# Mixture-of-experts in 64-row blocks, two side by side on the halves of TensorE's columns, the second block's weights copied to a fixed place by VectorE

## Chip, cores and metric

One core of one Trainium2 chip. The metric is the device time in microseconds of one execution; the median of three runs stands for a kernel. All data are fp32.

## What is computed

Two layers of a hybrid backbone over 512 latent and 256 context tokens of width 1024. Each layer has a token mixer (windowed attention, gated DeltaNet, latent attention) and then a mixture of experts. Layer 0 sends all 768 tokens through the experts, layer 1 only the 512 latent ones. The change lies in the experts:

```
swiglu(t, wg, wu, wd) = (silu(t @ wg) * (t @ wu)) @ wd      # 1024 -> 256 -> 1024
top_idx, top_w = route(h)          # 8 of 64 experts per token
for each expert: y = swiglu(rows that chose it); routed[token] += weight * y
out = swiglu(h, shared weights) + routed
```

The given inputs fix the routing. Of layer 0's 6144 rows, 12 experts get at most 64, 40 get 65 to 128, and 12 get 129 to 192. Of layer 1's 4096 rows the same three classes hold 41, 17 and 5 experts, and one expert has 219. In blocks of 128 rows of one expert that is 76 and 70 blocks; in blocks of 64 it is 128 and 94.

## The kernel before

Rows are sorted by expert into blocks of 128 rows (`phase_tail` computes, on the chip, a table `plan` with the expert of every block and the index list `idx`). `phase_experts` then runs a loop on each engine over pairs of blocks, `r = 0, 1`. A block goes through these steps:

- POOL gathers 128 rows of 1024 from DRAM (`gather`, L2214), two blocks ahead; TensorE turns them (`turn`, 8 transposes, L2227), ScalarE copies them to `xT` (L2282).
- `gate_up(r)` (L2233): 8 matmuls, 128 rows x 512 columns of gate and up weights, which TensorE takes as 16 passes. ScalarE applies silu, VectorE multiplies by the up half into `hid` (L2327, L2331), `turn_hidden` (L2239) turns it, VectorE copies it to `hT` (L2329, L2333).
- `down(r, n)` (L2244): 4 matmuls, 8 passes. ScalarE copies the left half of the result, VectorE the right half (L2338), ScalarE's queue stores 512 KB to `y_slots`.

TensorE's order in a pair is: gate_up(0), turn(0), gate_up(1), turn_hidden(0), turn(1), turn_hidden(1), down(0), down(1).

The weights of expert `e` (2 MB gate and up, 1 MB down) lie in slot `e % 4` of a ring `W` of `WRING = 4` slots. SP loads them in order of the experts; three are loaded before the loop. A slot is free when the last block of expert `e - 4` has ended: SP waits for `blocks_done`, which the last matmul of `down(r, 1)` raises, against the table `T_FREE`. One expert has at least one block, so a pair of blocks touches at most two experts, and the other two slots can be filled ahead.

The modulation product (L241) already uses groups of TensorE's columns: 8 matmuls with 2 stationary columns each, on column groups starting at 0, 32, 64 and 96 in turn, all with 128 rows and 512 moving columns of their own.

Of the kernel before, what the change touches and what calls it, by code (L numbers as in the profile page):

```python
# [50 lines left out]
BIG = 1e30  # L51

# [4 lines left out]


# [127 lines left out]
ARENA_WORDS = 53200  # L186
# [4 lines left out]
def plan_at(nq):  # L191

    n = nq * TOPK + NE + 2
    return n, 2 * n, 2 * n + NE + 1


def build(nc, A, out):
# [8 lines left out]
    NBMAX = NT + NT * TOPK + NE  # L206
# [3 lines left out]
    with outer:  # L210
# [48 lines left out]
        FIXED = max(b for a, b in arena.used)  # L259
        ROOMS = (NT * GCH + 6 * NTOK, (4 + 2 * MH) * NTOK + NT * MH * HD)  # L260
# [140 lines left out]
        def front_rows(featroom):  # L401

            first = carve(featroom)
            return first(NT, D), first(D), first(2, D)


        class Next:
# [3 lines left out]
            def __init__(self, stack):  # L411
                nq = NLT
                sizes = [nq * TOPK, nq * TOPK, nq * TOPK + NE + 2, plan_at(nq)[2], NT * 12, ROOMS[0], NT * W_VB, ROOMS[1]]
                self.at = max(b for a, b in arena.used if b <= FIXED) + sum(n + n % 2 for n in sizes)
                self.hT = sbuf(stack, "hT", [P, DK, NTOK], place=self.at)
                self.wt = arena.tensor[0:P, self.at + DK * NTOK:self.at + DK * NTOK + DK * 384]
                self.sems = Sems(nc, "next")
                self.x_out, self.w_in = self.sems("x_out"), self.sems("w_in")


        def phase_front(l, nq, vb, featroom, lateroom, X, x_in, nxt):
# [4 lines left out]
            xt, sq, hh = front_rows(featroom)  # L426
# [15 lines left out]
            with st:  # L442
# [43 lines left out]
                with nc.Block() as block:  # L486
# [306 lines left out]
                    def _(pe):  # L793
                        def item(it):
# [4 lines left out]
                            if kind == "chan":  # L799
                                c, jj = a // 3, a % 3  # L800
                                pe.wait_ge(w_in[c], 16)
                                w = wt[:, WOFF[c]:WOFF[c] + DK * 384].rearrange("p (k n) -> p k n", n=384)
# [793 lines left out]
        def phase_tail(l, nq, ob, W, dest, wk, idx, plan, route_keep, xg, gathered, xT, xT_ready, sz, w_in, c_in, T):  # L1596
# [6 lines left out]
            NB = nq * TOPK + NE  # L1603
            NBC = NB + 2
            T_SLOT, T_FREE, T_END = plan_at(nq)
# [5 lines left out]
            with st:  # L1611
# [32 lines left out]
                cmpb = sbuf(st, "cmpb", [NE, P])  # L1644
# [5 lines left out]
                bo = [ap[:, 0:TOPK * NB].rearrange("p (k n) -> p k n", n=NB) for ap in (xt[2], tt)]  # L1650
# [21 lines left out]
                with nc.Block() as block:  # L1672
# [168 lines left out]
                    def _(pe):  # L1841
# [94 lines left out]
                        def block_experts():  # L1936
                            pe.wait_ge(cmp_ready, 1)
                            nc.tensor.matmul(psum[0:1, 1, 0:P], cst("ones")[0:NE, 0:1], cmpb[:, :], start=True, stop=True).then_inc(be_done, 1)

                        def slot_tokens(i):  # L1940
# [3 lines left out]
                            for k in range(TOPK):  # L1944
                                n = i * TOPK + k
                                last = nc.tensor.matmul(psum[:, 0, 0:NB], po[:, i % 2, k], bo[i % 2][:, k], start=(n == 0), stop=(n == nq * TOPK - 1))
# [53 lines left out]
                    def _(dve):  # L2000
# [102 lines left out]
                        for j in range(1, nq):  # L2103
                            ch(V.scalar_tensor_tensor(out=nblk[:, :], in0=cnt, scalar=j * P + 0.5, in1=nblk[:, :], op0=ALU.is_gt, op1=ALU.add))
# [4 lines left out]
                        ch(V.tensor_scalar(tmpe[:, :], tmpe[:, :], float(P), nq * P + 1.0, ALU.mult, ALU.add))  # L2109
# [17 lines left out]
                        V.tensor_scalar(cmpb[:, :], cst("iota")[0:NE], ecol[:, 0:1], None, ALU.is_ge).then_inc(cmp_ready, 1)  # L2127
# [3 lines left out]
                        for i in range(nq):  # L2131
                            if i >= 2:
                                dve.wait_ge(hot_used, i - 1)
                            V.tensor_tensor(po[:, i % 2], cst("iota").unsqueeze(1).to_broadcast([P, TOPK, P]),
                                            p8[:, i].unsqueeze(2).to_broadcast([P, TOPK, P]), ALU.is_equal)
                            V.tensor_tensor(bo[i % 2], cst("iota")[:, 0:NB].unsqueeze(1).to_broadcast([P, TOPK, NB]),
                                            b8[:, i].unsqueeze(2).to_broadcast([P, TOPK, NB]), ALU.is_equal).then_inc(same_ready, 1)
                        ch(V.memset(idx[:, NB:NBC], 0))
# [3 lines left out]
                        V.tensor_copy(idx[:, 0:NB], psum[:, 0, 0:NB]).then_inc(idx_done, 1)  # L2142

                        ch(V.memset(bf[:, NB:NBC], float(NE)))
                        ch(V.tensor_scalar(bf[:, T_SLOT:T_SLOT + NBC], bf[:, 0:NBC], -1.0, None, ALU.add))
                        ch(V.tensor_copy(qi[:, :], bf[:, T_SLOT:T_SLOT + NBC]))
                        ch(V.tensor_scalar(qi[:, :], qi[:, :], WRING - 1, None, ALU.bitwise_and))
                        ch(V.tensor_copy(bf[:, T_SLOT:T_SLOT + NBC], qi[:, :]))
                        ch(V.tensor_scalar(bf[:, T_SLOT:T_SLOT + NBC], bf[:, T_SLOT:T_SLOT + NBC], float(WSLOT), None, ALU.mult))
# [3 lines left out]
                        ch(V.tensor_scalar(plan[:, T_END - 1:T_END], plan[:, T_END - 1:T_END], 1, None, ALU.logical_shift_right))  # L2153
# [6 lines left out]
        def phase_experts(l, nq, W, idx, plan, xs, ys, wk, route_keep, xg, gathered, xT, xT_ready):  # L2160
            NB = nq * TOPK + NE
            T_SLOT, T_FREE, T_END = plan_at(nq)
            st, S = ExitStack(), Sems(nc, f"ex{l}")
            with st:
                sg = sbuf(st, "sg", [P, 2, DE])
                hid = sbuf(st, "hid", [P, 2, DE])
                hT = sbuf(st, "hTe", [P, 2, DE])
                yb = sbuf(st, "yb", [P, 2, D])
                w_in = [S(f"w_in{r}") for r in range(WRING)]
                y_out = [S("y_out0"), S("y_out1")]  # L2170
                step = S("step")
                w_ready, blocks_done = S("w_ready"), S("blocks_done")
# [3 lines left out]
                rows_in = S("rows_in")  # L2176
                LEFT, RIGHT = (5, 7), (6, 5)

                def used_pairs(eng):

                    return eng.value_load(plan[0:1, T_END - 1:T_END], min_val=0, max_val=NB // 2)

                with nc.Block() as block:
                    @block.sync
                    def _(sp):
                        sp.sem_inc(w_ready, 3)
                        for e in range(3, NE):
                            r = e % WRING
                            if e >= WRING:
                                free = sp.value_load(plan[0:1, T_FREE + e - WRING:T_FREE + e - WRING + 1], min_val=1, max_val=NB + 1)  # L2190
                                sp.wait_ge(blocks_done, free)
                            sp.dma_start(W[:, r * WSLOT:r * WSLOT + DK * 2 * DE],
                                         A["w_gu"][l * (NE + 1) + 1 + e].rearrange("p k n -> p (k n)")).then_inc(w_in[r], 16)
                            sp.dma_start(W[:, r * WSLOT + DK * 2 * DE:(r + 1) * WSLOT],
                                         A["w_dn"][l * (NE + 1) + 1 + e].rearrange("p k n -> p (k n)")).then_inc(w_in[r], 16)
                            if e > 3:
                                before = e - 1
                                sp.wait_ge(w_in[before % WRING], 32 * (before // WRING + (before % WRING == 3)))
                                sp.sem_inc(w_ready, 1)
                        sp.wait_ge(w_in[(NE - 1) % WRING], 32 * (NE // WRING))  # L2200
                        sp.sem_inc(w_ready, 1)
                        sp.dma_start(xs[:, :, :], xres[0:nq * P, :].rearrange("(i p) d -> p i d", p=P)).then_inc(rows_in, 16)
                        sp.dma_start(ys[:, :, :], y_dram[0:nq * P, :].rearrange("(i p) d -> p i d", p=P)).then_inc(rows_in, 16)
# [4 lines left out]
                    def _(pool):  # L2208
# [9 lines left out]
                        for j in range(NB // 2):  # L2218
# [5 lines left out]
                    def _(pe):  # L2224
# [5 lines left out]

                        def gate_up(r, slot):
# [456 lines left out]
```

## Time and profile before

| | |
|---|---|
| median of 3 runs | 3626.09 us (3623.57 to 3629.45) |
| profiled execution, span | 3630.5 us |
| TensorE busy | 3384.4 us, 93% of the span |
| weight loads of TensorE | 1937.8 us, 53% |
| VectorE, ScalarE busy | 1088.2 us, 891.0 us |
| mean granted clock of TensorE | 0.964 of 2.4 GHz |
| HBM | 776.58 MB moved, mean 214 GB/s |

The span runs from the first to the last instruction of one profiled execution. No device time is shown apart from the span for that execution; its span is 4.4 us (0.12%) above the median of the runs. The expert loops take 981 to 1873 us (layer 0) and 2743 to about 3570 us (layer 1) of it.

### The profile page before, as it was taken

To read this page: it belongs to the slowest core of one execution; us is meant where nothing else is said; L and a number is where in the kernel's file an instruction comes from. 1 tells how busy PE (TensorE), PEld (TensorE's weight loads), DVE (VectorE), ACT (ScalarE), POOL (GpSimd) and SP (SyncE) were. 2 spreads that over 40 slices of the span, in tenths; PEclk is the share of its full clock that TensorE was granted. 3 is DMA by queue.
4 is the path that set the end of the run, shared out by engine and by line. 5 is a ranking of instruction groups with operands and counts; after the bars stand their busy time and mean duration, and the time that the engine had idled before them with its cause. 6 is when DMAs were issued, how large, how long until landed. Compare 5 with 4: busy or idle time off the path is not lost. (4 is left out here: it accounts for less than half of the span.)

```text
span 3630.5 us, 59980 instructions
## 1 busy us (share of the span) xinstructions
PE 3384.4 (93%) x22912; PEld 1937.8 (53%) x22913; DVE 1088.2 (30%) x2570; ACT 891.0 (25%) x1790; POOL 513.5 (14%) x568
## 2 busy tenths in 40 slices
PE   7998979989899999999987998899898999999996
PEld 4545659845444444444433555679544444444442
DVE  3424534445311111111125435434442111111114
ACT  2323432222211111111124224422221111111112
POOL 0100024220100000000024010052311000000003
PEclk8998989999999999999999999999899999999998
DMA  9603310123288886978867103200335999999965
GB/s 381 266 9 121 136 49 4 62 108 155 106 318 327 325 351 226 363 294 328 330 264 254 64 9 130 71 3 4 144 151 199 366 365 366 362 363 362 356 242 220
DMA packets 147619, 776.58 MB, mean 214 GB/s; under 512 B 25952, under 2 KB 43872, under 8 KB 110688
## 3 DMA queue, kind: packets, MB, share of 16 engines
q1 hardware_dynamic: 88960, 560.92, 39.7%
q0 software_dynamic: 33120, 120.60, 9.5%
q10 hardware_dynamic: 25344, 92.29, 6.2%
q8 instruction: 143, 2.34, 0.3%
q14 instruction: 52, 0.43, 0.0%
HBM read 637.44 MB, written 136.31 MB: 213 GB/s over the span
## 5 line engine op out<-in xcount | busy, mean ns | idle before, releaser
L2233 PE MATMUL psum<-arena 128*128 x2336 | 1037.5, 597 | 15.7 <-issue 15.7
L2233 PEld LDWEIGHTS psum<-arena 128*128 128x128 f32 x2336 | 433.8, 191 | 555.7 <-issue 555.7
L2244 PE MATMUL psum<-arena 128*128 x1168 | 515.3, 594 | 0.0
L810 PE MATMUL psum<-arena 128*128 128x480 f32 (+3 forms) x1088 | 401.5, 525 | 13.2 <-PEq L152 5.2
L2214 POOL DMA_INDIRECT arena<-h,arena x146 | 137.6, 943 | 1527.8 <-PE psum L2227 1503.7
L2244 PEld LDWEIGHTS psum<-arena 128*128 128x128 f32 x1168 | 215.9, 190 | 244.5 <-issue 244.4
L2294 ACT ACTIVATE arena<-psum 128x256 f32<-128x256 f32 x146 | 56.2, 385 | 1032.3 <-PE psum L2233 1032.3
L810 PEld LDWEIGHTS psum<-arena 128*128 128x128 f32 x1088 | 206.7, 193 | 186.8 <-issue 175.4
L2338 DVE COPY arena<-psum 128x512 f32<-128x512 f32 x146 | 101.0, 692 | 422.0 <-PE psum L2244 422.0
L2329 DVE COPY arena<-psum 128x256 f32<-128x256 f32 x73 | 31.0, 425 | 519.9 <-PE psum L2239 519.9
L2327 DVE TENSOR_TENSOR arena<-arena,psum 128x256 f32<-128x256 f32 x73 | 30.7, 421 | 488.0 <-ACT arena L2294 488.0
L2282 ACT COPY arena<-psum 128x1024 f32<-128x1024 f32 x146 | 147.9, 1013 | 87.2 <-PE psum L2227 87.2
L2301 ACT COPY arena<-psum 128x512 f32<-128x512 f32 x146 | 85.7, 587 | 291.2 <-PE psum L2244 291.2
L2227 PEld LDWEIGHTS psum<-arena 128*128 128x128 f32 x1168 | 134.4, 141 | 38.5 <-issue 38.5
L2227 PE MATMUL psum<-arena 128*128 128x128 f32 x1168 | 151.4, 273 | 0.0
L1864 PE MATMUL psum<-arena 128*128 128x512 f32 x320 | 143.1, 606 | 0.0
L996 PE MATMUL psum<-arena 128*128 128x64 f32 x896 | 120.1, 279 | 20.7 <-ACT arena L1108 20.2
L996 PEld LDWEIGHTS psum<-arena 128*128 128x128 f32 x896 | 109.5, 192 | 55.5 <-ACT arena L1108 40.0
L1432 DVE TENSOR_TENSOR arena<-psum,arena 128x384 f32<-128x384 f32 x120 | 66.9, 558 | 151.1 <-PE psum L1330 139.7
L2490 PE MATMUL psum<-arena 128*128 128x512 f32 x160 | 89.1, 658 | 22.4 <-DMA arena<-y_slots,arena 17.6
L2407 POOL DMA_INDIRECT arena<-y_slots,arena x80 | 88.2, 1103 | 107.1 <-POOLq L152 81.4
L1864 PEld LDWEIGHTS psum<-arena 128*128 128x128 f32 x320 | 61.6, 195 | 75.2 <-issue 75.2
(350 smaller groups left out, 3812.5 us busy)
## 6 DMA issues: line engine op xcount, KB each, us to landing
arena<-in_w_gu SPq DMA_DIRECT2D x130, 2048.0 KB
arena<-in_w_dn SPq DMA_DIRECT2D x130, 1024.0 KB
y_slots<-arena ACTq DMA_DIRECT2D x156, 512.0 KB
arena<-in_ada SPq DMA_DIRECT2D x24, 2048.0 KB
y_slots<-arena SPq DMA_DIRECT2D x8, 4096.0 KB
arena<-in_w_gdn SPq DMA_DIRECT2D x6, 1536.0 KB
arena<-in_w_out SPq DMA_DIRECT2D x2, 4096.0 KB
arena<-in_w_tok SPq DMA_DIRECT2D x4, 1920.0 KB
```

The costliest lines, as they stand in the source:

```text
L810: last = nc.tensor.matmul(bank(n, wide), lhsT[:, k], rhs[:, k], start=(k == 0), stop=(k == DK - 1))
L996: last = nc.tensor.matmul(psum[:, OUT, (u % 2) * HD:(u % 2 + 1) * HD], ET[:, u % 2, c * P:(c + 1) * P], v, start=(c == 0), stop=(c == len( ...
L1864: last = nc.tensor.matmul(psum[:, y_bank(i) + n, :], cT[:, i % 2, k * P:(k + 1) * P], wo[:, k, n * 512:(n + 1) * 512], start=(k == 0), sto ...
L2214: nc.gpsimd.indirect_dma_start(xg[:, b % 2], None, h2_dram, bass.IndirectOffsetOnAxis(ap=idx[:, b:b + 1], axis=0)).then_inc(gathered[b % 2 ...
L2227: last = nc.tensor.transpose(psum[:, k // 4, (k % 4) * P:(k % 4 + 1) * P], xg[:, r, k * P:(k + 1) * P], cst("ident"))
L2233: last = nc.tensor.matmul(psum[:, 2 + r, :], xT[:, r, k * P:(k + 1) * P], W[:, bass.ds(slot + k * 2 * DE, 2 * DE)], start=(k == 0), stop=( ...
L2244: last = nc.tensor.matmul(psum[:, (LEFT, RIGHT)[n][r], :], hT[:, r, j * P:(j + 1) * P], W[:, bass.ds(slot + DK * 2 * DE + j * D + n * 512, ...
L2282: nc.scalar.copy(xT[:, r].rearrange("p (b n) -> p b n", b=2), psum[:, 0:2, :]).then_inc(xT_ready, 1)
L2301: nc.scalar.copy(yb[:, r, 0:512], psum[:, LEFT[r], :]).then_inc(ys_ready, 1)
L2338: nc.vector.tensor_copy(yb[:, r, 512:D], psum[:, RIGHT[r], :]).then_inc(yv_ready, 1)
L2407: nc.gpsimd.indirect_dma_start(G[:, n % NG], None, y_dram, bass.IndirectOffsetOnAxis(ap=dest[:, i, k:k + 1], axis=0)).then_inc(gathered[n ...
L2490: last = nc.tensor.matmul(psum[:, i % 2, :], dg[:, i % 2, k], G[:, n % NG, H:D], start=False, stop=(k == TOPK - 1))
```

## The change

Blocks have 64 rows. Two consecutive blocks, which may belong to two experts, form a unit of 128 rows that goes through the old steps. Only the matmuls with weights are split: block `half(0)` uses columns 0 to 63 of TensorE and writes PSUM partitions 0 to 63, block `half(1)` the others. The first block reads its weights in the ring, at an address from the table. The second reads a copy at a fixed place (`late_gu[r]`, `late_dn[r]`), which VectorE makes during the pair before. The ring keeps four slots, and a slot is free when the unit with the last block of its expert has ended. The number of units is `(nq*8*2 + 64)/2` at most; those that are used are 64 in layer 0 and 47, rounded up to 48, in layer 1, where the blocks before were 76 and 70.

```diff
 def gate_up(r, slot):
     for k in range(DK):
-        last = nc.tensor.matmul(psum[:, 2 + r, :], xT[:, r, k * P:(k + 1) * P], W[:, bass.ds(slot + k * 2 * DE, 2 * DE)],
+        nc.tensor.matmul(psum[half(0), 2 + r, :], xT[:, r, rows_of(k, 0)], W[:, bass.ds(slot + k * 2 * DE, 2 * DE)],
+                         start=(k == 0), stop=(k == DK - 1))
+        last = nc.tensor.matmul(psum[half(1), 2 + r, :], xT[:, r, rows_of(k, 1)], late_gu[r][:, k * 2 * DE:(k + 1) * 2 * DE],
                                 start=(k == 0), stop=(k == DK - 1))
...
                             for r in range(2):
                                 b = 2 * i + r
-                                pe.wait_ge(w_ready, need[r])
+                                wait_weights(pe, need[r])
+                                pe.wait_ge(lgu_ready, b + 1)
...
+                            pe.wait_ge(ldn_ready, 2 * i + 1)
                             down(0, 0, slot[0], left_done)
...
+    def copy_gu(r, slot):
+        nc.vector.tensor_copy(late_gu[r][:, :], W[:, bass.ds(slot, GU)]).then_inc(lgu_ready, 1)
+
+    def copy_dn(r, slot):
+        nc.vector.tensor_copy(late_dn[r][:, :], W[:, bass.ds(slot + GU, DN)]).then_inc(ldn_ready, 1)
...
                             for r in range(2):
                                 b = 2 * i + r
+                                need, slot = late[r]
+                                if r == 0:
+                                    wait_weights(dve, need)
+                                    copy_gu(r, slot)
                                 dve.wait_ge(blocks_done, b + 2)
                                 dve.wait_ge(y_out[r], 16 * i + 16)
-                                nc.vector.tensor_copy(yb[:, r, 512:D], psum[:, RIGHT[r], :]).then_inc(yv_ready, 1)
+                                nc.vector.tensor_copy(yb[r][:, 512:D], psum[:, RIGHT[r], :]).then_inc(yv_ready, 1)
+                                if r == 1:
+                                    wait_weights(dve, need)
+                                    copy_gu(r, slot)
+                                copy_dn(r, slot)
...
-                        for j in range(1, nq):
-                            ch(V.scalar_tensor_tensor(out=nblk[:, :], in0=cnt, scalar=j * P + 0.5, in1=nblk[:, :], op0=ALU.is_gt, op1=ALU.add))
+                        for j in range(1, nq * HALVES):
+                            ch(V.scalar_tensor_tensor(out=nblk[:, :], in0=cnt, scalar=j * BR + 0.5, in1=nblk[:, :], op0=ALU.is_gt, op1=ALU.add))
...
-                        ch(V.tensor_scalar(bf[:, T_FREE:T_FREE + NE], ends[0:1, :], 1.0, None, ALU.add))
+                        ch(V.tensor_scalar(bf[:, T_FREE:T_FREE + NE], ends[0:1, :], 3.0, None, ALU.add))
...
+                        ch(V.tensor_scalar(plan[:, T_FREE:T_FREE + NE], plan[:, T_FREE:T_FREE + NE], 1, None, ALU.logical_shift_right))
```

The room for the copies comes from `xs` and `ys`, which the combine step reads: SP now loads them into slots 0 and 1 of the ring after experts 60 and 61 have ended. Before, it loaded them to a place of their own once the last weights had landed. The routing in `phase_tail` gets a few more short steps on VectorE for the longer tables.

On TensorE a pair starts, in the kernel before, with rows of this kind (L2233 is gate_up, L2227 turn, ISA a register step that sets the address in the ring):

```order
L2233 ISA
L2233 MATMUL psum<-arena 128x512
L2233 ISA
L2233 MATMUL psum<-arena 128x512
L2264 ISA
L2265 REGISTER_ALU
L2227 MATMUL psum<-arena 128x128 x8
```

After the change the same place reads (L2274 is the first block's matmul, L2276 the second's, L2265 turn):

```order
L2274 ISA
L2274 MATMUL psum<-arena 64x512
L2276 MATMUL psum<-arena 64x512
L2274 ISA
L2274 MATMUL psum<-arena 64x512
L2276 MATMUL psum<-arena 64x512
L2311 ISA
L2312 REGISTER_ALU
L2265 MATMUL psum<-arena 128x128 x8
```

Each matmul has become two, one for each half of the columns, and the whole-width transposes still stand between them.

On VectorE the end of a pair was, before (L2331 and L2333 make the second block's `hid` and `hT`, L2338 copies the right halves of the two results; ISA steps carry waits):

```order
L2331 TENSOR_TENSOR arena<-arena,psum 128x256
L2333 COPY arena<-psum 128x256
L2337 ISA
L2338 COPY arena<-psum 128x512
L2336 REGISTER_ALU
L2338 COPY arena<-psum 128x512
```

and is after the change (L2376 is the wait for the weights and the copy of gate and up, L2379 the copy of down, L2405 the copy of a right half):

```order
L2394 TENSOR_TENSOR arena<-arena,psum 128x256
L2396 COPY arena<-psum 128x256
L2376 ISA
L2376 COPY arena<-arena 128x4096
L2404 ISA
L2405 COPY arena<-psum 128x512
L2379 ISA
L2379 COPY arena<-arena 128x2048
L2403 REGISTER_ALU
L2405 COPY arena<-psum 128x512
L2376 ISA
L2376 COPY arena<-arena 128x4096
```

The copy for the next pair's first unit, with its wait for that unit's weights, now stands ahead of both copies of results; the one for the second unit stands behind them.

## Rows read from the trace of the kernel before

**Rows 1.** Page: busy us, share of the span, instructions of each engine.

```profile
PE 3384.4 (93%) x22912; PEld 1937.8 (53%) x22913; DVE 1088.2 (30%) x2570; ACT 891.0 (25%) x1790; POOL 513.5 (14%) x568
```

**Rows 2.** Page: costliest groups (busy us, mean ns; idle before and releaser).

```profile
L2233 PE MATMUL psum<-arena 128*128 x2336 | 1037.5, 597 | 15.7 <-issue 15.7
...
L2214 POOL DMA_INDIRECT arena<-h,arena x146 | 137.6, 943 | 1527.8 <-PE psum L2227 1503.7
```

**Rows 3.** Windows: busy us of PE, PEld, DVE, ACT, POOL; clock, DMA share, GB/s.

```profile
1100.00:1400.00 300.00, 299.31 (x882) 144.09 (x880) 38.06 (x77) 51.61 (x78) 24.63 (x26) 1.00 0.82 320
...
3100.00:3400.00 300.00, 300.00 (x885) 144.64 (x884) 38.68 (x78) 51.55 (x78) 24.35 (x26) 1.00 0.92 363
```

**Rows 4.** Timeline of TensorE over one pair (start, us, group).

```profile
1470.22 7.11 PE L2233 MATMUL psum<-arena 128*128 x16
...
1478.04 7.03 PE L2233 MATMUL psum<-arena 128*128 x16
...
1486.41 7.06 PE L2244 MATMUL psum<-arena 128*128 x16
1493.31 7.11 PE L2233 MATMUL psum<-arena 128*128 x16
```

**Rows 5.** Timeline around one modulation product on four column groups.

```profile
323.75 0.59 PE L980 MATMUL psum<-arena 128*128 128x256 f32 x2
...
324.27 0.11 PEld L241 LDWEIGHTS psum<-arena 128*2 128x2 f32 x8 [0.33 <-issue]
324.27 1.90 PE L241 MATMUL psum<-arena 128*2 128x512 f32 x16
...
326.10 1.10 PE L996 MATMUL psum<-arena 128*128 128x64 f32 x8
```

**Rows 6.** Groups by form: a weight load of 64 columns.

```profile
L845 PEld LDWEIGHTS psum<-arena 128*64 128x64 f32 x10 | 1.2, 118 | 0.0
```

**Rows 7.** Groups by form on VectorE.

```profile
L2338 DVE COPY arena<-psum 128x512 f32<-128x512 f32 x146 | 101.0, 692 | 422.0 <-PE psum L2244 422.0
...
L2025 DVE TENSOR_TENSOR arena<-arena 128x1024 f32<-128x1024 f32 x10 | 12.2, 1225 | 0.3
...
L704 DVE TENSOR_SCALAR arena<-arena 128x1024 f32<-128x1024 f32 x8 | 6.0, 752 | 1.1 <-POOL arena L531 1.1
```

**Rows 8.** Page: transfers, KB each.

```profile
arena<-in_w_gu SPq DMA_DIRECT2D x130, 2048.0 KB
arena<-in_w_dn SPq DMA_DIRECT2D x130, 1024.0 KB
y_slots<-arena ACTq DMA_DIRECT2D x156, 512.0 KB
```

**Rows 9.** Timeline of SP, layer 1: two loads are issued.

```profile
3019.87 0.33 SPq L2192 DMA_DIRECT2D arena<-in_w_gu  x1
...
3023.67 0.45 SPq L2194 DMA_DIRECT2D arena<-in_w_dn  x1
```

**Rows 10.** Waits of SP in layer 1's expert loop: us in total, times, longest.

```profile
SPq L2199 <- DMA arena<-in_w_dn: 224.4, 28, 8.2
...
SPq L2201 <- DMA arena<-in_w_dn: 11.6, 1, 11.6
```

**Rows 11.** Windows: while loads are under way, and one pair.

```profile
3019.87:3042.98 23.11, 23.11 (x69) 11.13 (x68) 2.98 (x6) 3.97 (x6) 1.87 (x2) 1.00 0.92 363
3022.00:3040.00 18.00, 18.00 (x57) 8.87 (x57) 2.29 (x5) 2.87 (x5) 1.61 (x2) 1.00 0.98 408
```

**Rows 12.** Timeline: TensorE after a pause.

```profile
783.94 1.97 PE L1844 MATMUL psum<-arena 128*128 128x128 f32 x8 [4.62 <-DVE arena L2014]
```

**Rows 13.** Windows (last numbers: granted clock, DMA share, GB/s).

```profile
783.00:789.00 6.00, 5.06 (x12) 3.12 (x13) 3.28 (x5) 2.40 (x4) 0.78 (x2) 0.50 0.16 65
```

**Rows 14.** Timeline: the expert loop of layer 0 starts.

```profile
976.82 0.06 DVE L2314 MEMSET arena<- 128x2 f32 x1
...
981.00 8.79 PE L2233 MATMUL psum<-arena 128*128 x16 [7.08 <-issue]
```

More of the change, by code:

```diff
@@ L1936, in block_experts @@
                         def block_experts():
-                            pe.wait_ge(cmp_ready, 1)
-                            nc.tensor.matmul(psum[0:1, 1, 0:P], cst("ones")[0:NE, 0:1], cmpb[:, :], start=True, stop=True).then_inc(be_done, 1)
+                            pe.wait_ge(cmp_ready, -(-NB // P))
+                            nc.tensor.matmul(psum[0:1, 1, 0:NB], cst("ones")[0:NE, 0:1], cmpb[:, :], start=True, stop=True).then_inc(be_done, 1)
                         def slot_tokens(i):
@@ L1945, in slot_tokens @@
                                 n = i * TOPK + k
-                                last = nc.tensor.matmul(psum[:, 0, 0:NB], po[:, i % 2, k], bo[i % 2][:, k], start=(n == 0), stop=(n == nq * TOPK - 1))
+                                last = nc.tensor.matmul(psum[:, 0, 0:NU], po[:, i % 2, k], bo[i % 2][:, k], start=(n == 0), stop=(n == nq * TOPK - 1))
                             last.then_inc(hot_used, 1)
@@ L2189, in _ @@
                             if e >= WRING:
[L2190 removed]
+                                free = sp.value_load(plan[0:1, T_FREE + e - WRING:T_FREE + e - WRING + 1], min_val=1, max_val=NU + 1)
                                 sp.wait_ge(blocks_done, free)
+                            sp.wait_ge(w_in[e % 2], 32 * (e // 2))
                             sp.dma_start(W[:, r * WSLOT:r * WSLOT + DK * 2 * DE],
[L2193 removed]
+                                         A["w_gu"][l * (NE + 1) + 1 + e].rearrange("p k n -> p (k n)")).then_inc(w_in[e % 2], 16)
                             sp.dma_start(W[:, r * WSLOT + DK * 2 * DE:(r + 1) * WSLOT],
[L2195 to L2203, printed above, removed]
+                                         A["w_dn"][l * (NE + 1) + 1 + e].rearrange("p k n -> p (k n)")).then_inc(w_in[e % 2], 16)
+                        for r in range(2):
+                            sp.wait_ge(w_in[r], 32 * (NE // 2))
+                        for r, (rows, source) in enumerate(((ys, y_dram), (xs, xres))):
+                            free = sp.value_load(plan[0:1, T_FREE + NE - WRING + r:T_FREE + NE - WRING + r + 1], min_val=1, max_val=NU + 1)
+                            sp.wait_ge(blocks_done, free)
+                            sp.dma_start(rows, source[0:nq * P, :].rearrange("(i p) d -> p i d", p=P)).then_inc(rows_in, 16)
                         sp.wait_ge(rows_in, 32)
@@ L2216, in gather @@
                                                          ).then_inc(gathered[b % 2], 16)
-                        for j in range(NB // 2):
+                        for j in range(NU // 2):
                             with pool.If(pairs > j):
@@ L2243, in down @@
                             for j in range(2):
-                                last = nc.tensor.matmul(psum[:, (LEFT, RIGHT)[n][r], :], hT[:, r, j * P:(j + 1) * P],
-                                                        W[:, bass.ds(slot + DK * 2 * DE + j * D + n * 512, 512)],
+                                c = j * D + n * 512
+                                nc.tensor.matmul(psum[half(0), (LEFT, RIGHT)[n][r], :], hT[r][:, rows_of(j, 0)], W[:, bass.ds(slot + GU + c, 512)],
+                                                 start=(j == 0), stop=(j == 1))
+                                last = nc.tensor.matmul(psum[half(1), (LEFT, RIGHT)[n][r], :], hT[r][:, rows_of(j, 1)], late_dn[r][:, c:c + 512],
                                                         start=(j == 0), stop=(j == 1))
@@ L2359, in phase_combine @@
                 xnew = lambda i: nxt.xlast[:, i - NLT] if nxt and i >= NLT else xs[:, i]
+                G = [sbuf(st, f"G{h}", [P, TOPK, D]) for h in range(NG // TOPK)]
                 rows = sbuf(st, "rows3", [P, 2, D])
@@ L2489, in _ @@
                                 pe.wait_ge(gathered[n % NG], 16 * (n // NG) + 16)
-                                last = nc.tensor.matmul(psum[:, i % 2, :], dg[:, i % 2, k], G[:, n % NG, H:D], start=False, stop=(k == TOPK - 1))
+                                last = nc.tensor.matmul(psum[:, i % 2, :], dg[:, i % 2, k], G[i % 2][:, k, H:D], start=False, stop=(k == TOPK - 1))
                             last.then_inc(summed, 1)
```

188 lines of the change are left out of this document (115 added, 73 removed).

## Prediction

> **What bounds the kernel now.** The page first: TensorE is busy 93% of the span [rows 1]. The costliest groups come next: gate_up alone takes 1037.5 us, and the gathers count 146 blocks [rows 2]. The windows say where. In 300 us of either layer's expert loop TensorE is busy 299 to 300 us at clock 0.99 to 1.00, VectorE 38 and ScalarE 52, while DMA moves 320 and 363 GB/s at a share of 0.82 and 0.92 [rows 3]. So both loops are bound by TensorE, and in layer 1 DMA stands close behind. The timeline gives the unit of price: a pair takes 1493.31 - 1470.22 = 23.1 us, a block 11.55; gate_up(1) starts 7.8 into the pair, the four downs take 6.9 [rows 4]. A pass of 512 columns takes (7.8 - 0.9)/16 = 0.43 us.
>
> **What is removed.** 146 blocks become 64 + 48 = 112 units. If a unit costs what a block does, that is 34 x 11.55 = 393 us less. It rests on two halves of the columns working at the same time. The trace has such a case. The modulation product puts 16 passes of 512 columns on four column groups; they begin at 324.27 and the next group begins at 326.10, so they take 1.83 us [rows 5], where the same number of passes in gate_up takes 6.9. That is 3.75 of 4, each with moving columns of its own. Two halves should give nearly 2, so I take a unit's matmuls at the old time. The bounds are 1.0 and 2.0 times.
>
> All 8 weight loads of the first two passes per group there lie within 0.11 us, beside the matmuls [rows 5]. The Trainium skill says otherwise ("TensorE: Matmul & The Clock Gate", Part 3, The mechanism): a weight load overlaps matmuls in flight only when its row group differs, and all of these use all rows. By the row the loads cost nothing here; by the rule they stand in the open, and the change loses more than it saves (the price is a rival below).
>
> **Switching.** Whole-width transposes stand between split matmuls: six switches in a pair. Into the modulation product, 323.75 + 0.43 = 324.18 against 324.27, and out of it, 324.27 + 4 x 0.43 = 325.99 against 326.10 [rows 5]: 0.1 us each. 56 pairs x 6 x 0.1 = 34 us.
>
> **The copies.** A copy of 128x4096 within SBUF isn't in the trace. An operation with one source, 128x1024, takes 752 ns, one with two sources 1225; a copy out of PSUM, 128x512, 692 [rows 7]. At about 1 ns per element 4096 cost 4.4 us and 2048 2.3; at half that, from the 752 of the one-source row, 2.3 and 1.3. The copy has one source and both ends in SBUF, so I take 2.3 and 1.3. Per pair that is 7.2 us more on VectorE, which now works 3 us in 23 [rows 11]. Where weights are there in time the copy for the next unit 0 runs beside the downs (6.9 us), and the copy for unit 1 ends about 3 us into the next pair, 5 before it is needed: nothing. At the loop's start the first one, from 976.9 on, ends before TensorE's first matmul at 981.0 [rows 14]: nothing. If VectorE is late, its multiply into `hid` and its right-half copies queue behind it, and ScalarE's stores behind those.
>
> **The ring.** This is where the gain goes. A load of 3.1 MB [rows 8] issued at 3019.87 lands when SP, waiting 8.0 us on average after 3024.1, goes on: 12.2 us after its issue [rows 9, 10]. While loads are under way DMA moves 408 GB/s [rows 11], so each further load costs 7.7 us, or 8.7 at the 363 of a whole pair with its gathers and stores. Slots come free when a unit ends: 3.4 us before the next pair starts for unit 0 (half of the downs), at its start for unit 1. Before, a pair used two slots and the other two were filled ahead. Now a pair uses up to four, and `blocks_done` frees them at its end. From the counts of rows per expert I wrote down for every pair how many experts that its first unit needs, and how many that the pair needs, can only be loaded once units of the pair before have ended:
>
> - none: 22 pairs. No stall, 23.7 us.
> - (0, 1): 19 pairs (14 in layer 0). The load lands at 12.2 - 3.4 = 8.8 into the pair; the copy adds 2.3 and a semaphore 0.1. TensorE is ready at 7.9. Stall 3.4, in all 65.
> - (0, 2): 3 pairs, one load more at 8.7: stall 12.1, in all 36.
> - (1, 2): 3 pairs. TensorE stands, and the stores wait with it, so I take 1.8 to start plus 7.7: 9.5 - 3.4 + 2.3 = 8.4 (with company 11.1), in all 25.
> - (1, 3): 3 pairs, 8.4 and then 9: 52.
> - (2, 2) and (2, 3): 4 pairs, 8.4 + 7.9 = 16.3: 65.
> - (2, 4): 2 pairs, 16.3 + 10: 53.
>
> Together 296 us, 230 of them in layer 1, 66 in layer 0. SP is late first, VectorE's wait for weights second (it holds back the right half of unit 0 and so its store), TensorE third.
>
> **The clock.** After 4.6 us of idle TensorE starts at 783.94 [rows 12] at clock 0.50, that is 1.2 instead of 2.4 GHz, in the whole window to 789 [rows 13]: half of at least 5.1 us is lost, 2.6 to 2.9. Twenty stalls above are 8 us or longer: 20 x 2.8 = 56. The 19 short ones lose between nothing and 2.8; I take 1.5: 28. The slower pass lies inside the loop load, unit, free slot, so it isn't absorbed.
>
> **Small things.** The routing gains ten short VectorE steps and loses columns in its one-hot tables; the loop has two more waits and loads of registers per pair: 5 us. `xs` and `ys` are issued about a pair before the end instead of two or three; their 6.3 MB take 16 us of the last 23: nothing.
>
> **The sum.** -393 + 34 + 296 + 84 + 5 = +26, near +30 with the few stalls that push a later pair into a short one (4). Against the profiled span 3630.5 that is 3660; the median stands 4.4 lower, so 3656. By layer: layer 0 saves 12 blocks (139) and pays about 66 + 19 + 28 + 3 = 116; layer 1 saves 22 (254) and pays 304.
>
> **The rivals.** A measurement of this kernel tells 0.2%, 7 us, from no change.
>
> 1. As forecast, slower: 3656, own range 3634 to 3710. Chance 0.48.
> 2. The loads come faster than priced, and the kernel is faster. If DMA kept 440 GB/s with loads always waiting, a load would cost 7.1 instead of 7.7 to 8.7 and land 1 us earlier: the 19 short stalls shrink to 2.4 and cost no clock (-19 - 28), the 15 long ones by 1 to 3 each (-30): 3656 - 77 = 3580. It decides once a load with company lands in less than 11.3 us. For it: short windows touch such rates; against it: the mean of 18 us is 408 [rows 11]. Chance 0.25.
> 3. The copies run at one element at a time, 4.4 and 2.3 us. Every stall of the 34 pairs grows by 2.1, twice where both units wait, and the short ones then lose the clock too: 34 x 2.1 + 9 + 19 x 1.3 = 105: 3760. For it: every copy in the trace (PSUM) runs so; against it the 752 ns row. Chance 0.10.
> 4. The halves overlap badly. A weight load of 64 columns takes 118 ns [rows 6]; 48 of them per unit in the open cost 112 x 48 x 0.118 = 634 us: 4290. With no overlap at all it would be 112 x 24 x 0.43 = 1156 more. This is the mechanism of the rule cited above; the row on four column groups speaks against it. A tenth of a pass pitch would already give +100. Chance 0.08.
> 5. Gains and stalls cancel within 7 us: 0.09.
>
> Likeliest is the first: 3656. The range must leave out no more than 2 in 10. Below, half of rival 2 fits above 3590; above, rival 1's tail and most of rival 3 lie below 3750. Range 3590 to 3750. Faster by over 0.2%: 0.25, same 0.09, slower 0.66.
>
> **What the profile will show.** 112 gathers of x instead of 146. The split gate_up near 6.9 us for 32 passes; a pitch over 0.25 us per pass would be rival 4. VectorE's 128x4096 copy near 2.3 us; 4.4 is rival 3. In layer 0 most pairs at 23.7 us and some 27 to 30; in layer 1 stretches with pairs of 42 to 54, where TensorE idles some 230 us, VectorE waits on DMA of the weights and the clock shows 0.5 after each pause. Layer 0's loop should get shorter by some 20 us, layer 1's longer by 50. The prediction is wrong if a load issued at a unit's end lands much sooner or later than 12 us, if pauses don't halve the clock, or if TensorE idles although weights are there.

## The result, and the profile after

The changed kernel takes 3725.55 us (median; 3724.18 to 3731.42), the kernel before 3625.75 beside it: ratio 1.0278, 95% interval 1.0264 to 1.0293. It is slower by 100 us, where 30 were forecast. The profiled execution has a span of 3722.9 us.

The page of the kernel after (busy us, share, instructions; then groups with busy us, mean ns | idle before and releaser), against [rows 1, 2]:

```profile
PE 3094.3 (83%) x24444; PEld 1636.1 (44%) x24445; DVE 1427.8 (38%) x2720; ACT 820.8 (22%) x1688; POOL 558.3 (15%) x534
...
L2274 PE MATMUL psum<-arena 128*64 x1792 | 867.5, 641 | 399.1 <-issue 204.7
L2276 PE MATMUL psum<-arena 128*64 128x512 f32 x1792 | 868.3, 641 | 0.0
...
L2376 DVE COPY arena<-arena 128x4096 f32 x116 | 266.4, 2297 | 555.8 <-DMA arena<-in_w_dn 551.1
L2252 POOL DMA_INDIRECT arena<-h,arena x112 | 184.0, 1643 | 1582.3 <-PE psum L2265 1558.7
```

TensorE is busy 290 us less, so the saving was made; but it now stands idle for 399.1 us ahead of gate_up, where it was 15.7. VectorE waits 551 us for down weights. There are 112 gathers, and one takes 1643 ns instead of 943.

The two loops in windows (busy us of PE, PEld, DVE, ACT, POOL; clock, DMA share, GB/s), against [rows 3]:

```profile
984.60:1902.00 917.40, 792.64 (x3712) 290.29 (x3712) 321.58 (x335) 126.93 (x192) 117.56 (x62) 0.96 0.74 287
2772.00:3655.00 883.00, 617.32 (x2784) 227.06 (x2784) 244.11 (x255) 95.33 (x144) 59.33 (x46) 0.85 0.70 277
```

In layer 1 TensorE is idle 266 of 883 us and the clock has fallen to 0.85. DMA moves less than before as well (277 GB/s against 363): averaged over the loop no engine and no queue is at its limit, they wait for each other in turn. Inside a long wait it is DMA that is full: from 3130 to 3145 TensorE does nothing, and DMA runs at a share of 1.01 and 428 GB/s.

TensorE's timeline at the start of two pairs in a row of layer 0 that wait for no weights (start, us, group [idle before <-releaser]), against [rows 4]:

```profile
1128.42 0.64 PE L2274 MATMUL psum<-arena 128*64 x1 [1.56 <-issue]
1128.43 0.64 PE L2276 MATMUL psum<-arena 128*64 128x512 f32 x1
1128.90 0.59 PE L2274 MATMUL psum<-arena 128*64 x1
...
1153.77 0.64 PE L2274 MATMUL psum<-arena 128*64 x1 [1.55 <-issue]
1153.78 0.64 PE L2276 MATMUL psum<-arena 128*64 128x512 f32 x1
```

First and second half start 0.01 us apart, and the next pair of passes follows 0.48 later here, 0.43 in the rows after. So the halves work fully side by side, and the weight loads of gate_up, now 64 in a pair where there were 32, cost nothing visible. But the pair takes 1153.77 - 1128.42 = 25.35 us, not 23.7, and in each of them some 1.6 us pass in which TensorE waits for nothing but its own issue.

One of the pairs of the kind (0, 1), across the engines:

```profile
1029.69 2.92 POOL L2252 DMA_INDIRECT arena<-h,arena  x1 [7.32 <-PE psum L2265]
...
1030.20 2.28 DVE L2376 COPY arena<-arena 128x4096 f32 x1
...
1033.45 0.33 SPq L2232 DMA_DIRECT2D arena<-in_w_gu  x1
...
1038.71 0.64 PE L2274 MATMUL psum<-arena 128*64 x1 [1.87 <-issue]
...
1048.88 2.29 DVE L2376 COPY arena<-arena 128x4096 f32 x1 [11.30 <-DMA arena<-in_w_dn]
...
1051.49 1.11 PE L2274 MATMUL psum<-arena 128*64 x1 [4.67 <-DMA arena<-in_w_dn]
...
1052.39 1.06 PE L2274 MATMUL psum<-arena 128*64 x1
```

The slot comes free and SyncE issues the load at 1033.45; it is in at 1048.88, when the copy begins; gate_up(1) follows 2.6 us later, at half clock (0.90 between passes; the granted clock is 0.50 from 1051.49 to 1055). The pair itself began at 1038.71. The load took 15.4 us where I had priced 12.2, and ahead of it GpSimd's gather took 2.92 us, beside VectorE's copy.

### The profile page after: what moved, and what is told of

The parts are those of the page before. It is cut to its first block and busy times, and to the rows that moved or that the text cites. A ratio compares the mean times of both kernels' runs of the same rounds, so it can differ in the third digit from the quotient of the medians.

```text
span 3722.9 us, 63767 instructions
## 1 busy us (share of the span) xinstructions
PE 3094.3 (83%) x24444; PEld 1636.1 (44%) x24445; DVE 1427.8 (38%) x2720; ACT 820.8 (22%) x1688; POOL 558.3 (15%) x534
## 5 line engine op out<-in xcount | busy, mean ns | idle before, releaser
L2274 PE MATMUL psum<-arena 128*64 x1792 | 867.5, 641 | 399.1 <-issue 204.7
L2276 PE MATMUL psum<-arena 128*64 128x512 f32 x1792 | 868.3, 641 | 0.0
L2274 PEld LDWEIGHTS psum<-arena 128*64 128x64 f32 x1792 | 254.0, 148 | 955.3 <-issue 955.3
L2376 DVE COPY arena<-arena 128x4096 f32 x116 | 266.4, 2297 | 555.8 <-DMA arena<-in_w_dn 551.1
L2252 POOL DMA_INDIRECT arena<-h,arena x112 | 184.0, 1643 | 1582.3 <-PE psum L2265 1558.7
L2290 PE MATMUL psum<-arena 128*64 128x512 f32 x896 | 396.6, 595 | 0.0
L2288 PE MATMUL psum<-arena 128*64 x896 | 396.5, 595 | 0.0
L826 PEld LDWEIGHTS psum<-arena 128*128 128x128 f32 x1088 | 208.0, 194 | 188.5 <-issue 176.6
L2276 PEld LDWEIGHTS psum<-arena 128*64 128x64 f32 x1792 | 253.5, 147 | 0.0
L2288 PEld LDWEIGHTS psum<-arena 128*64 128x64 f32 x896 | 118.1, 137 | 232.5 <-issue 232.5
L1880 PE MATMUL psum<-arena 128*128 128x512 f32 x320 | 142.0, 602 | 0.0
L2379 DVE COPY arena<-arena 128x2048 f32 x116 | 141.4, 1219 | 0.0
L1012 PEld LDWEIGHTS psum<-arena 128*128 128x128 f32 x896 | 109.2, 192 | 55.6 <-ACT arena L1124 39.9
L2331 ACT COPY arena<-psum 128x1024 f32<-128x1024 f32 x112 | 113.5, 1013 | 84.5 <-PE psum L2265 84.5
L2265 PE MATMUL psum<-arena 128*128 128x128 f32 x896 | 119.2, 276 | 0.0
L2265 PEld LDWEIGHTS psum<-arena 128*128 128x128 f32 x896 | 98.7, 141 | 45.4 <-issue 45.4
```

The source lines that it names most:

```text
L826: last = nc.tensor.matmul(bank(n, wide), lhsT[:, k], rhs[:, k], start=(k == 0), stop=(k == DK - 1))
L1012: last = nc.tensor.matmul(psum[:, OUT, (u % 2) * HD:(u % 2 + 1) * HD], ET[:, u % 2, c * P:(c + 1) * P], v, start=(c == 0), stop=(c == len( ...
L1880: last = nc.tensor.matmul(psum[:, y_bank(i) + n, :], cT[:, i % 2, k * P:(k + 1) * P], wo[:, k, n * 512:(n + 1) * 512], start=(k == 0), sto ...
L2252: nc.gpsimd.indirect_dma_start(xg[:, b % 2], None, h2_dram, bass.IndirectOffsetOnAxis(ap=idx[:, b:b + 1], axis=0)).then_inc(gathered[b % 2 ...
L2265: last = nc.tensor.transpose(psum[:, k // 4, (k % 4) * P:(k % 4 + 1) * P], xg[:, r, k * P:(k + 1) * P], cst("ident"))
L2274: nc.tensor.matmul(psum[half(0), 2 + r, :], xT[:, r, rows_of(k, 0)], W[:, bass.ds(slot + k * 2 * DE, 2 * DE)], start=(k == 0), stop=(k == ...
```

## The experiments

Each time stands beside the kernel before on the same chip. "Against after" is the difference of the ratios to the kernel before, times 3626. The texts set off by a bar were written before each run.

| run | median us | ratio, 95% interval | against after |
|---|---|---|---|
| e1_two_loads | 3685.62 | 1.0155 (1.0130 to 1.0179) | -45 |
| e2_before_six_loads | 3734.91 | 1.0298 (1.0279 to 1.0316) | (before +108) |
| e3_no_copies | 3582.80 | 0.9873 (0.9855 to 0.9890) | -147 |
| e4_no_loads | 3385.18 | 0.9330 (0.9301 to 0.9360) | -344 |
| e9_no_loads_two_registers | 3260.09 | 0.8977 (0.8962 to 0.8992) | -472 |
| e5_gu_alone | 3646.45 | 1.0052 (1.0035 to 1.0068) | -82 |
| e6_copy_later | 3675.12 | 1.0129 (1.0112 to 1.0145) | -54 |
| e7_early_release | 3722.09 | 1.0268 (1.0249 to 1.0287) | -4 |
| e8_all | 3507.93 | 0.9669 (0.9653 to 0.9685) | -221 |
| e10_no_release | 3508.24 | 0.9661 (0.9644 to 0.9677) | -224 |
| e11_split_slot | 3457.73 | 0.9522 (0.9506 to 0.9538) | -274 |

My theory after the trace was threefold: the head of the loop (register loads), the landing of the loads with the copy behind it, and slots that are held too long. The rival for each was that it is hidden by the others.

**The head of the loop, from the changed kernel.**

```diff
-                                need = [weights(pe, 2 * i + r) for r in range(2)]
...
-                                    wait_weights(pe, need[r])
```

> The changed kernel, but TensorE no longer loads the four registers that say which weights must be in (VectorE, which waited for the same unit's weights before it copied, already covers them): two register loads a pair instead of six. Theory A (the head of the loop costs: six loads of some 0.75 us run longer than the queued matmuls cover, 1.95 us idle at the start of a pair): pairs that wait for nothing fall from 25.5 to about 23.6 us; the time falls by at least 22 pairs x 1.9 = 40 us and at most 54 x 1.9 = 103 us, so 3625 to 3685 us. Theory B (the excess over the forecast is only in the weights' landing): under 10 us, 3715 to 3730 us.

45 us less: theory A at the weak end of its range. The two loops got shorter by 28 and 11 us. The starts of the same two pairs now:

```profile
1122.79 0.59 PE L2274 MATMUL psum<-arena 128*64 x1
...
1146.37 0.59 PE L2274 MATMUL psum<-arena 128*64 x1
```

23.58 us and no idle time, what the forecast had (23.7). But a (0, 1) pair gains nothing:

```profile
1031.45 0.33 SPq L2232 DMA_DIRECT2D arena<-in_w_gu  x1
...
1046.63 2.29 DVE L2374 COPY arena<-arena 128x4096 f32 x1 [11.05 <-DMA arena<-in_w_dn]
...
1049.07 1.11 PE L2274 MATMUL psum<-arena 128*64 x1 [6.34 <-DVE arena L2374]
```

The 1.87 us at the start of this pair and the 4.67 ahead of its gate_up(1) have become one wait of 6.34. The register loads cost time in pairs whose weights are there, and are hidden in the others: 22 pairs x 1.77 (25.35 - 23.58) = 39.

**The same from the kernel before.**

```diff
+                                more = [pe.value_load(plan[0:1, bass.ds(2 * i + r, 1)], min_val=1, max_val=NE) for r in range(2)]
...
+                                    pe.wait_ge(w_ready, more[r])
```

> The kernel before, with two more register loads and two more waits on TensorE in each pair and nothing else. Theory A: the loads go past what the queued matmuls cover, some 1.2 to 1.9 us for each of 74 pairs, +90 to +140 us, 3715 to 3765 us. Theory B (register loads hide behind the queue): under +10 us.

108 us more: theory A. Gate_up in its timeline, against [rows 4]:

```profile
1475.64 7.13 PE L2233 MATMUL psum<-arena 128*128 x16 [1.25 <-issue]
...
1500.16 7.13 PE L2233 MATMUL psum<-arena 128*128 x16 [1.25 <-issue]
```

A pair takes 24.52 instead of 23.09: two loads with their waits cost 1.43 us, 0.7 each. With four loads no pair but the first of each loop had more than 0.44 us of idle time at its start (15.7 us in all [rows 2]), so the matmuls still queued cover four, and the fifth and sixth are paid for. That four lie just within the cover is argued: no run has three or five, and none has loads without their waits.

**The copies.** Inside the loop a write of two elements a partition stands for each copy, so the second halves use stale weights.

```diff
-                                        copy_gu(r, slot)
+                                        nc.vector.memset(late_gu[r][:, 0:2], 0.0).then_inc(lgu_ready, 1)
...
-                                    copy_dn(r, slot)
+                                    nc.vector.memset(late_dn[r][:, 0:2], 0.0).then_inc(ldn_ready, 1)
```

> The changed kernel without VectorE's copies of the second halves' weights inside the loop (a write of two elements a partition stands in their place and signals as they did; the second halves then use stale weights). Theory A (the copies lie beside other work except where the weights land late, and there the 2.3 us copy of gate and up stands between landing and matmul): unstalled pairs stay at 25.3 to 25.6 us, the stalled ones (34 of 56) lose 2.3 us each, some -80 us, 3620 to 3670 us. Theory B (copies cost nothing at all): under 10 us. Theory C (the copies also slow the loads' landing, by the use of the memory they share): more than -120 us, under 3600 us.

147 us less: the size that theory C gave, so the copies cost more than their own 2.3 us on the path. Theory C's reason, the shared memory, is not shown by this run, and a run below speaks against it. A (0, 1) pair:

```profile
1030.91 0.95 POOL L2252 DMA_INDIRECT arena<-h,arena  x1 [7.31 <-PE psum L2265]
...
1034.67 0.33 SPq L2232 DMA_DIRECT2D arena<-in_w_gu  x1
...
1047.16 0.06 DVE L2408 MEMSET arena<- 128x2 f32 x1 [8.36 <-DMA arena<-in_w_dn]
```

The load is in after 12.5 us and the gather's issue takes 0.95 again. 12.5 is near the price that I had (12.2); with the copies it was 15.4. In layer 0 thirteen of the fourteen (0, 1) pairs take 25 to 27 us; in the kernel after eleven of the fourteen took 31 to 33.

**No loads.** SyncE waits for the slots and signals at once; the blocks use old weights. Once with six register loads, once with two.

```diff
+                            if e >= WRING:
+                                sp.sem_inc(w_in[e % 2], 32)
+                                continue
```

> The changed kernel without the loads of the experts from number 4 on inside the loop (SyncE waits for the slots as before and signals at once; the blocks use old weights). Theory A (the loop's loss is stalls on weights and the clock behind them, 368 us above 56 x 25.5): all pairs near 25.5 us, 3725 - 368 = 3357 us, 3330 to 3385. Theory B (a good part of the long pairs is VectorE's, ScalarE's or the gathers' doing): 3450 us or more.

> The run without the experts' loads (from number 4 on; the blocks use old weights), with two register loads a pair on TensorE instead of six: the block work alone, as the forecast summed it. Theory A (a unit of two 64-row blocks costs the forecast 11.85 us, and the register loads the rest of the 25.5 us pair): 3385 - 56 x 1.9 = 3280 us, 3260 to 3300; the forecast without its terms for stalls, clock and small things is 3271 us. Theory B (a further cost per pair is hidden in the register loads' time): 3320 us or more.

344 and 472 us less: theory A both times, once at the slow end of its range (3385) and once at the fast end (3260). The second is the block work alone. The groups of gate_up in both:

```profile
L2277 PE MATMUL psum<-arena 128*64 x1792 | 818.1, 611 | 117.2 <-issue 91.1 <-SPq L2233 14.8 <-DVE arena L2379 11.4
```

```profile
L2277 PE MATMUL psum<-arena 128*64 x1792 | 795.5, 597 | 15.4 <-DVE arena L2377 15.4
```

With two register loads every pair but the first of each layer takes 23.6 or 23.7 us, in both layers, and the idle time is that of the loops' starts. The difference between the two, 128 us or 2.3 a pair, is the price of the four loads where nothing else hides them: 102 us of it is idle time (117.2 - 15.4), and gate_up's busy time is 23 us longer (818.1 against 795.5). Of the 128, only 45 show in the real kernel.

**Gate and up weights waited for alone.** Semaphores for them apart from those of the down weights, on SyncE, VectorE and TensorE:

```diff
-                w_in = [S("w_even"), S("w_odd")]
+                w_gu, w_dn = [S("gu_even"), S("gu_odd")], [S("dn_even"), S("dn_odd")]
...
-                                        wait_weights(dve, need)
+                                        wait_weights(dve, need, w_gu)
...
+                                    wait_weights(dve, need, w_dn)
```

> The changed kernel with one pair of semaphores for the gate and up weights and one for the down weights, so that VectorE copies a second half's gate and up weights as soon as they are in (the median load of them landed after 11.7 us, that of the down weights after 14.8). Theory A (in the stalled pairs the landing of the down weights is what the copy of gate and up waits for): 3.1 us less in each of 34 stalled pairs, some -100 us, 3590 to 3660 us. Theory B (the slot that comes free late sets the stall, so that the next loads are late by the same): under -30 us.

82 us less. TensorE itself still waits here for both kinds ahead of gate_up. The waits (us in total, times, longest):

```profile
PE psum L2278 <- DMA arena<-in_w_dn: 183.2, 30, 14.7
PE psum L2278 <- issue: 88.3, 44, 8.8
PE psum L2278 <- DVE arena L2380: 51.2, 4, 14.7
```

So the copy now runs while the down weights land, and the landing of these is what TensorE waits for: theory A (82 of its 100 us). What this last wait keeps back was not measured by itself.

**The first copy moved.**

```diff
-                                    if r == 0:
-                                        wait_weights(dve, need)
-                                        copy_gu(r, slot)
                                     dve.wait_ge(blocks_done, b + 2)
                                     dve.wait_ge(y_out[r], 16 * i + 16)
                                     nc.vector.tensor_copy(yb[r][:, 512:D], psum[:, RIGHT[r], :]).then_inc(yv_ready, 1)
-                                    if r == 1:
-                                        wait_weights(dve, need)
-                                        copy_gu(r, slot)
+                                    wait_weights(dve, need)
+                                    copy_gu(r, slot)
```

> The changed kernel with VectorE's first gate and up copy of a pair moved behind the copy of the first unit's right half, some 3.4 us later, so that it no longer lies on the second gather's issue by GpSimd (2.92 us beside the copy, 0.95 alone). Theory A (the late gather's transfers fall into the next load's time: that load took 15.4 us to land with the copies and 12.5 without them): gathers back to some 0.95 us, the load of a stalled pair lands in 12.5 us, some 2 to 3 us less in each of 34 pairs, -60 to -100 us, 3625 to 3665 us. Theory B (the slow gather is hidden by its own queue): within 15 us, or slower by the copies that now end later.

54 us less, 10 us above the top of theory A's range, and all of it in layer 0, whose loop is shorter by 51. In layer 1 the copy that now ends later is paid at the start of the long pairs, as theory B had it: waits of 9.4 and 16.8 us there became 10.9 and 18.1. The same pair as above once more:

```profile
1026.38 0.95 POOL L2252 DMA_INDIRECT arena<-h,arena  x1 [7.32 <-PE psum L2265]
...
1030.14 0.33 SPq L2232 DMA_DIRECT2D arena<-in_w_gu  x1
...
1042.49 2.29 DVE L2376 COPY arena<-arena 128x4096 f32 x1 [7.62 <-DMA arena<-in_w_dn]
```

12.35 us from issue to landing, with every copy still made, so the copies do not slow the load by themselves. The edit moves VectorE's wait for the weights too, but in the pair of the kernel after the first copy has no idle time before it, so that wait held nothing back there. What moved beside the load is the gather (q0). DMA between issue and landing, first of the kernel after, then here (packets, MB, share):

```profile
q1 hardware_dynamic: 359, 4.31, 72.2%
q10 hardware_dynamic: 282, 1.04, 16.5%
q0 software_dynamic: 136, 0.49, 10.8%
```

```profile
q1 hardware_dynamic: 313, 3.56, 76.1%
q10 hardware_dynamic: 233, 0.89, 17.5%
q0 software_dynamic: 8, 0.01, 0.3%
```

With the gather's issue slowed by 2 us its 0.49 MB fall into the load's time; otherwise they are over before it. The other gather of the pair now lies beside the second copy (2.62 us, at 1043.42), after the load has landed. 0.49 MB are 1.3 us at the 379 GB/s of the window. That the rest of the 3 us comes from the next load's bytes on the same queue (q1, 0.75 MB more) is argued; a run that moves nothing but the gather wasn't made.

**The early release.** SyncE waits for two tables (the last unit whose weights TensorE reads in the slot, the last one that is copied out of it):

```diff
+                    done = sp.value_load(plan[32:33, T_FREE + e:T_FREE + e + 1], min_val=1, max_val=NU + 1)
+                    copied = sp.value_load(plan[0:1, T_FREE + e:T_FREE + e + 1], min_val=1, max_val=NU + 1)
+                    sp.wait_ge(blocks_done, done)
+                    sp.wait_ge(ldn_ready, copied)
```

> The changed kernel, but a slot whose expert has one block only, and that a second half, is free for the next load as soon as VectorE has copied it out, and not when the unit is done (SyncE waits on two tables: last unit that TensorE reads, last unit that is copied). Theory A (stalls come from slots that are held by experts that nobody reads any more): such experts free their slot a pair (25 us) earlier; with 27 pairs of the stalled kind in both layers, -50 to -150 us, 3575 to 3675 us. Theory B (the slot of another expert in the same pair, which TensorE reads directly, is what each stall waits for): within 20 us.

Nothing, within the noise: theory B. The trace shows why: in layer 0 all loads are issued at the same points of their pairs as in the kernel after, within 2 us, so the rule lets hardly any load start earlier. That this is because loads are issued in the order of the experts, and the slot before it in that order is still read by TensorE, is argued.

**All together, and without the release.**

> All of it together: two register loads on TensorE, gate and up weights waited for alone, the first copy moved behind the right half, each gate and up copy in two pieces that TensorE waits for apart, and the early release. Theory A (head of the loop, landing plus copy, and the held slots are the loss): -40 - 100 - 60 - 50 at least, if they add, 3475 us; overlaps between them leave 3430 to 3560 us, below the kernel before by 2% or more. Theory B (they remove the same stall, and the loads' bandwidth of layer 1 sets the rest): 3580 to 3640 us.

> The version of all the edits together, without the early release (alone it gave 3 us). Theory A (with the head, the landing and the gathers mended, the release still does nothing, since loads are issued in order and the slot before it in the row is held): within 15 us of that version's 3508. Theory B (the release counts once the copies no longer end late): 20 to 60 us slower, 3530 to 3570 us.

3508 both times, 3.3% under the kernel before, inside theory A's range. The release does nothing here either. The single edits add up to 185 us (45, 82, 54, 4) and together give 221. The gate and up copy in two pieces was in no run by itself, so how much of the difference is its own stays open. Layer 0 now has 26 of its first 31 pairs at 23.6 us; its loop, from the first pair's start to the last's, fell from 889 to 754 us, layer 1's from 856 to 778.

**Slots in two parts.**

```diff
+                        load_gu(3)
+                        for e in range(4, NE):
+                            load_gu(e)
+                            load_dn(e - 1)
+                        load_dn(NE - 1)
```

where `load_gu(e)` waits for the gate_ups of the slot's last unit (`gu_done`) and `load_dn(e)` for its downs (`blocks_done`), both for the copies.

> The version of all the edits together, and each slot in two parts: the gate and up weights of the next expert are loaded as soon as the last gate and up matmuls that read the slot are done (some 7 to 15 us into a pair), the down weights, issued after the next expert's gate and up weights, when the downs are done (17 to 20 us into it). Theory A (the long pairs of layer 1 are a row: pair, slots free at its end, four loads of 3.15 MB, pair): two thirds of the bytes start 10 us earlier, the fourteen pairs of 40 us and more lose 8 to 12 us each, -80 to -150 us, 3360 to 3430 us. Theory B (the loads' bandwidth sets those pairs: four loads are 30 us at 420 GB/s, with gathers and stores 35): under -40 us.

50 us less than e10_no_release and 53 less than e8_all: between the two theories, outside the range of A. The loop of layer 1, first in e8_all, then here:

```profile
2628.00:3425.00 797.00, 607.95 (x2763) 226.73 (x2765) 244.25 (x298) 94.17 (x143) 45.26 (x47) 0.87 0.77 307
```

```profile
2620.00:3375.00 755.00, 605.65 (x2760) 237.98 (x2762) 242.15 (x298) 93.44 (x142) 43.86 (x47) 0.89 0.82 324
```

The five pairs of 49 to 51 us fell to 35 to 39, 67 us together. But the pair behind each of them grew by 5 to 11 us, 36 together: part of the wait was passed on and not removed. DMA went from 307 to 324 GB/s. Four loads of 3.15 MB at the 363 GB/s of [rows 3] would take 35 us (an estimate), so the longest pairs now lie near the loads' own time. This version beats the kernel before by 4.8% (0.9522).

## Why the prediction was wrong

The forecast was 30 us slower, and the kernel is 100 us slower. The gap to the block work alone (e9_no_loads_two_registers) is 472 us; the forecast had 385 for it: stalls 296, clock 84, small things 5. The idle time ahead of gate_up gives 399 - 15 = 384 of the 472, and the other 88 are the lower clock and what hangs on it.

- **What is removed, Switching: right.** The forecast without stalls, clock and small things is 3656 - 385 = 3271 us; measured 3260. The halves overlap fully, a pair is 23.6 us (23.7 forecast). The row behind it was thin: the weight loads of [rows 5] have two columns each, those here 64, and only the runs show that these too cost nothing. Rival 4 is out. As for the rule of the Trainium skill that a weight load overlaps matmuls in flight only when its row group differs ("TensorE: Matmul & The Clock Gate", Part 3, The mechanism), the trace disagrees for 64-column loads into two column halves: 148 ns each, all rows, and the pitch stays 0.43 us. The same section also lets a load into the background weight buffer be pulled ahead of matmuls in flight; the prediction left that out, and the trace is in line with it.
- **The copies: right in their own price, wrong as "nothing".** They take 2.3 and 1.2 us (2.3 and 1.3 forecast), so rival 3 is out. The 2.3 was in part luck: 752 ns for 1024 elements, simply scaled, is 3.0 us, and the prediction gives no reason for less. And a copy costs more than VectorE's time: the gather's issue beside it is slower, which I had not looked for.
- **The ring: this step failed, in one term.** I took 12.2 us from issue to landing from a kernel in which no copy stood beside the gather. In the (0, 1) pair shown it is 15.2 (e1_two_loads) to 15.4 (after), and 12.35 once the first copy is moved off the gather (e6_copy_later). The forecast stall of such a pair was 3.4; with 3.0 more for the landing it is 6.4, and 6.34 is what e1_two_loads shows. That run has only two register loads in a pair, and its trace has nineteen waits of this kind, 2.9 to 6.9 us long, 110 us in all where 65 were forecast: 45 us too little. The rest of the term held. The classes came out as counted, 22 free pairs and fifteen with long waits, and the long waits of e1_two_loads add up to 232 us against the 231 forecast.
- **The clock: right.** 84 forecast; 88 is all that is left of the 472 beside the idle time, and 72 of it is gate_up's busy time (867.5 against 795.5 us).
- **Small things: this step failed too.** "Two more waits and loads of registers per pair" had no price of its own inside the 5 us. TensorE has six register loads in a pair where it had four, and they outlast the matmuls that are queued: 1.77 us in each of 22 pairs, 39 us, and 45 in the time of e1_two_loads.
- **By layer: wrong in layer 0.** From the first pair's start to the last one's, and a pair more, layer 0 went from 882 to 915 us, where 20 less were forecast; layer 1 from 812 to 882, where 50 more were. Layer 0 has 14 of the 19 (0, 1) pairs and most of the free ones, the two kinds whose price was off.

3656 - 11 for the block work + 45 + 39 = 3729, against 3726: the two terms make up the miss. Two of the prediction's own signs of being wrong came true, a landing later than 12 us and TensorE idle although the weights are there. The direction and rival 1 as the likeliest were right; the size was not, and 3726 lies 16 us above rival 1's own range.

## What to carry to other kernels

Count the register loads at the head of a hardware loop on the engine that is the bound, and ask how much queued work covers them: here the fifth and sixth cost 0.7 us each. A wait that another engine has already made for the same data needs no register of its own. When a ring becomes tight, price each load from the release of the slot to the first use, and free, load and wait for each part by itself: separate semaphores gave 82 us, a slot in two parts 50, and a finer rule for one kind of slot nothing. Copies that are "hidden" must be placed as well as counted: moving one by some 4 us (from 17.2 to 21.1 us into its pair) gave 54.

## What the runs showed of the hardware

- An indirect DMA's issue on GpSimd takes 0.94 to 0.95 us alone, and 2.6 to 2.9 beside VectorE's copy of 128x4096 within SBUF. Mean over all: 943 ns before, 1643 after, 986 in e8_all, where the first copy is moved and each is cut in two.
- That copy runs at 0.56 ns an element of a partition (2297 ns for 4096), more than twice the rate of the copy out of PSUM (692 ns for 512 elements [rows 7]).
- TensorE's passes on two halves of the columns, each with moving data of its own, start 0.01 us apart and keep the pitch of one (0.43 us), with 64-column weight loads of 148 ns beside them.
- Two more register loads from SBUF with their waits at the head of TensorE's loop made a pair 1.43 us longer (e2_before_six_loads), 0.7 each; four fewer made it 1.77 shorter (e1_two_loads).
